# Another plan of what the attention slots of layer 0 carry: a modulation batch over three slots, queries between batches, gating weights split beside queries

## The reference, cut to what matters

```python
def _modulation(cond, w, b):
    return jnp.split(jax.nn.silu(cond) @ w + b, 6, axis=-1)      # w: 1024 x 6144, twice (x and ctx), each layer
...
def _mixer_ab(h, hc, w_in, w_out, ...):                          # layer 0
    z = h @ w_in
    q, k, v = ...                                                # 8 query heads, 2 key heads of 64; q and k with rope
    u, gv = gelu(z[..., A_IN:A_IN + B_WIDTH]), gelu(z[..., A_IN + B_WIDTH:])   # 512 + 512 columns: the gating
    a_out = _window_attention(q, k, v, kc, vc, sink)             # each block of 128 queries: 3 blocks of keys + 256 of context
    b_out = _spatial_gating(u, gv, ...)
    y = concatenate([a_out, b_out]) @ w_out
```

## Time and profile before

| what | us |
|---|---|
| median of 3 runs | 3166.69 |
| lowest and highest | 3163.51, 3169.23 |
| the profiled execution: its time | 3168.14 |
| its span | 3166.4 |
| the 40 slots and the closing one of `stage_window` | from 120.51 to about 521.4 |

### The profile page before, as it was taken

The page is one execution under the profiler, slowest core; times in us unless marked ns, Lnnn a source line. Parts: engine busy times, 40 slices in busy tenths (PEclk is TensorE's granted clock), DMA queues, the critical chain, the costliest instruction groups (busy, mean ns, idle before and its releaser), DMA issues. The chain is left out here.

```text
span 3166.4 us, 40486 instructions
## 1 busy us (share of the span) xinstructions
PE 2816.2 (89%) x15572; PEld 2300.4 (73%) x15572; DVE 1376.0 (43%) x2155; ACT 881.3 (28%) x1669; POOL 519.5 (16%) x359
## 2 busy tenths in 40 slices
PE   5877986697999999999966999999696999999993
PEld 2654865585888888888855888888575888888882
DVE  3454543564333333333364555555563333333336
ACT  4223333243121211212115434443433221122211
POOL 0000000233121121212140000000033211222114
PEclk6889998798999999999986999999998999999997
DMA  6455123542011110101023111110352111111114
GB/s 223 175 222 200 54 67 112 166 126 87 27 43 36 35 44 26 53 26 53 26 93 111 36 46 34 48 34 8 107 126 87 52 41 43 49 53 53 40 47 112
DMA packets 193647, 239.42 MB, mean 76 GB/s; under 512 B 15976, under 2 KB 154816, under 8 KB 187392
## 3 DMA queue, kind: packets, MB, share of 16 engines
q1 hardware_dynamic: 193248, 237.81, 23.3%
q10 hardware_dynamic: 288, 0.10, 0.0%
HBM read 204.22 MB, written 37.88 MB: 76 GB/s over the span
## 5 line engine op out<-in xcount | busy, mean ns | idle before, releaser
L1830 DVE TENSOR_TENSOR y<-y,pair 128x1024 f32<-128x1024 f32 x288 | 351.1, 1219 | 338.5 <-PE pair L1882 338.5
L1880 PE MATMUL pair<-m_wbh,m_ath 128*128 128x512 f32 x1152 | 449.8, 390 | 4.6 <-DVE y L1830 4.5
L1882 PE MATMUL pair<-m_wbh,m_atl 128*128 128x512 f32 x1152 | 450.3, 391 | 0.0
L1881 PE MATMUL pair<-m_wbl,m_ath 128*128 128x512 f32 x1152 | 449.3, 390 | 0.0
L1858 DVE TENSOR_TENSOR m_atl<-m_sq,m_ath 128x512 fp32r<-128x512 f32 x160 | 102.3, 640 | 696.0 <-POOL m_sq L1815 696.0
L1798 ACT ACTIVATE m_rel<-pair 128x512 f32<-128x512 f32 x160 | 88.9, 555 | 1019.9 <-PE pair L1898 1019.9
L1815 POOL TENSOR_TENSOR m_sq<-m_rel 128x512 f32<-128x512 f32 x160 | 154.1, 963 | 1214.6 <-ACT m_rel L1798 1214.6
L1896 PE MATMUL pair<-hth,m0n_wah 128*128 128x512 f32 (+1 forms) x768 | 272.8, 355 | 13.3 <-POOL m0n_wal L1808 13.3
L1897 PE MATMUL pair<-htl,m0n_wah 128*128 128x512 f32 (+1 forms) x768 | 273.3, 356 | 0.0
L1898 PE MATMUL pair<-hth,m0n_wal 128*128 128x512 f32 (+1 forms) x768 | 273.2, 356 | 0.0
L1880 PEld LDWEIGHTS pair<-m_wbh,m_ath 128*128 128x128 f32 x1152 | 216.4, 188 | 52.8 <-DVE y L1830 7.5
(11 more groups left out here) (241 smaller groups left out, 5095.5 us busy)
## 6 DMA issues: line engine op xcount, KB each, us to landing
a_ring<-in_w_mod SPq DMA_DIRECT2D x40, 1024.0 KB, 10.5
m_rawa<-in_mlp_w SPq DMA_DIRECT2D x64, 512.0 KB, 4.2
m_rawb<-in_mlp_w SPq DMA_DIRECT2D x64, 512.0 KB, 4.2
x_rows<-r_res SPq DMA_DIRECT2D x28, 512.0 KB, 3.1
r_raw<-cat_cols SPq DMA_DIRECT2D x18, 512.0 KB, 4.7
m_rawa<-x_rows SPq DMA_DIRECT2D x18, 512.0 KB, 3.7
mod_w<-in_w_mod SPq DMA_DIRECT2D x8, 1024.0 KB, 12.2
r_xin<-in_x SPq DMA_DIRECT2D x16, 512.0 KB, 3.7
```

What stands on the lines that cost most here:

```text
L1830: dve.tensor_tensor(k.y[:, t, :], k.y[:, t, :], k.pair[t % 2][:, :], ALU.add).then_inc(s_y, 1)
L1880: pe.matmul(o, ath[:, m, ts], wbh[:, m, cols], start=m == 0, stop=False)
L1881: pe.matmul(o, ath[:, m, ts], wbl[:, m, cols], start=False, stop=False)
L1882: i = pe.matmul(o, atl[:, m, ts], wbh[:, m, cols], start=False, stop=m == M - 1)
```

## The change

It replaces the tables. A batch of modulation is cut in parts of 3, 3 and 2 chunks that three slots in a row carry; `mod_rows` and the turn come in the third. The five batches start at slots 0, 4, 8, 13 and 17 (before: whole in slots 2, 7, 11, 14 and 17). The queries of the next two `it` go between the batches, at 3, 7, 11, 12, 16 and 20 (before 5, 9, 12, 15, 19, 22). The query weights are split at the ends of slots 1, 11 and 21 (before 1, 13, 23), and the gating parts at the ends of 20, 21, 30 and 31, two at each (before 18, 19, and four at 31). The gates start at slot 22 (before 20).

| slots | before | after |
|---|---|---|
| 0 to 2 | -, -, mod 1 | mod 1 in three parts |
| 3 to 7 | -, -, q, -, mod 2 | q, mod 2 in three parts, q |
| 8 to 12 | -, q, -, mod 3, q | mod 3 in three parts, q, q |
| 13 to 19 | -, mod 4, q, -, mod 5, -, q | mod 4 in three parts, q, mod 5 in three parts |
| 20 to 24 | gate, gate, q + gate, gate, gate | q, -, gate, gate + gate, gate |
| 25 to 31 | q + gate, gate, gate, gate, q, gate, q | q + gate, gate, gate, gate, q + gate, gate, q |
| 32 to 39 | ten gates, two each in 35 and 37 | ten gates, two each in 34 and 37 |

```diff
-    q_slot = {(1, 0): 5, (1, 1): 9, (1, 2): 12, (2, 0): 15, (2, 1): 19, (2, 2): 22, (3, 0): 25, (3, 1): 29, (3, 2): 31}
+    q_slot = {(1, 0): 3, (1, 1): 7, (1, 2): 11, (2, 0): 12, (2, 1): 16, (2, 2): 20, (3, 0): 25, (3, 1): 29, (3, 2): 31}
...
-    for b, n in ((1, 2), (2, 7), (3, 11), (4, 14), (5, 17)):
-        first[n], second[n] = ("mod", b), ("turn", b)
-    gates = [20, 21, -22, 23, 24, -25, 26, 27, 28, 30] + [32, 33, 34, 35, -35, 36, 37, -37, 38, 39]
+    parts = ((0, 3), (3, 6), (6, KT))
+    batch_slot = {1: 0, 2: 4, 3: 8, 4: 13, 5: 17}
+    for b, n in batch_slot.items():
+        for i, (lo, hi) in enumerate(parts):
+            first[n + i] = ("mod", b, lo, hi)
+        second[n + 2] = ("turn", b)
+    gates = [22, 23, -23, 24, -25, 26, 27, 28, -29, 30] + [32, 33, 34, -34, 35, 36, 37, -37, 38, 39]
...
-    q_splits = {1: 1, 13: 2, 23: 3}
-    gate_splits = {18: (0, 1), 19: (2, 3), 31: (4, 5, 6, 7)}
+    q_splits = {1: 1, 11: 2, 21: 3}
+    gate_splits = {20: (0, 1), 21: (2, 3), 30: (4, 5), 31: (6, 7)}
...
-    chunk_slot = lambda i: {1: 2, 2: 7, 3: 11, 4: 14, 5: 17}[i // KT + 1]
+    chunk_slot = lambda i: batch_slot[i // KT + 1] + i % KT // 3
...
-            def modulation(b):
-                for kt in range(KT):
+            def modulation(b, begin, end):
+                for kt in range(begin, end):
...
                 if f:
-                    beside_free(before)
+                    if f[0] != "mod" or f[2] == 0:
+                        beside_free(before)
```

More of the change, by code:

```diff
@@ L608, in stage_window @@
     bank_of = lambda g: k.bank[g % 4] if g < HEAD else BESIDE
-    rotated_at = {n + 1: g for n, (x, g) in ((n, f) for n, f in first.items() if f[0] == "q") if turned(g)}
+    rotated_at = {n + 1: f[1] for n, f in first.items() if f[0] == "q" and turned(f[1])}
     parted_at = {n + 1: g for n, g in rotated_at.items()}
@@ L690, in beside @@
             def beside(f):
-                kind, i = f
+                kind, i = f[0], f[1]
                 if kind == "gate":
@@ L711, in _ @@
                         chunk(i)
-                if n in first and first[n][0] == "mod":
+                if n in first and first[n][0] == "mod" and first[n][3] == KT:
                     b = first[n][1]
@@ L1145, in _ @@
                     else:
-                        modulation(f[1])
+                        modulation(*f[1:])
                 if n:
```

## The result

Two numbers for the same change:

| | before | after |
|---|---|---|
| median of 5 runs | 3163.51 us (3158.52 to 3169.23) | 3138.50 us (3134.53 to 3143.66) |
| profiled execution | 3168.14 us | 3139.57 us |

The account below looks back on a forecast made before the run. TensorE was taken as the busiest engine, with winnable idle time in slots 0 to 19 and 32. Terms -32.2 + 7.6 - 7.8 + 2.6 = -29.8 us gave 3138.3 profiled, 3137 median; range 3128 to 3153, own range 3129 to 3146.

Parts of the forecast that it names:

- Slots 0 to 19: Modulation batches in three parts and moved queries: 154.1 us against 186.3, so -32.2 us.
- The wait that takes the place of the DMA's: Part-two modulation slots: TensorE waits for VectorE's copies, behind rotate; maxima starts 2.7 us into the slot, not 1.2.
- The first slots: Slots 0 to 2: 23.9 us against 31.5, with 1.2 GHz only in slot 0 and half of slot 1.
- Slots 20 to 31: Moved gating and query splits delay maxima and gates, less slot 20's old wait: +7.6 us in sum.
- Slot 32: Gating parts 4 and 5 split a slot earlier: 13.6 us against 21.35, so -7.8 us.
- The clock in parts two and three: Ten modulation slots with idle stretches of 1.9 to 2.3 us: one clock fall in ten, +2.6 us, bounds 0 and 26.
- The rival of 18 us: Micro-idles pull the clock down in eight of ten modulation slots: 18 us given back, 3155 us; chance 0.15.
- batch 2's stretches: Old plan's modulation slot: TensorE idle stretches up to 1.87 us left the clock at 1.00; taken as evidence against falls.
- Late ring: Chunks land at the worst time and each batch keeps half its waits: 13 us, 3150 us; chance 0.12.
- slower: The clock stays at 1.2 GHz through all modulation slots: 61 us more, 3198 us; chance 0.04.
- no effect: The plan does not reach the end because another chain ends the stage: 3167 us; chance 0.04.
- One sign: If the forecast is right, DMA share is even over slots 0 to 19; before, 0.84 in a modulation slot, 0.12 beside.

Follow-up runs that it names:

- experiments 3 and 4: Modulation chunks load a quarter of their bytes, same matmuls: in the old plan 3133.72 us, in the new plan 3142.28 us.
- the other three profiles of these slots: New plan run again (3143.18 us), new plan with gating parts 4 to 7 all split at slot 31 (3146.19 us), new plan with quarter chunks (3142.28 us).
- Experiment 5: New plan with modulation chunks after the transposes and VectorE's and ScalarE's copies before normalise and exponents: 3119.23 us, ratio 0.9854 to the kernel before.
- the second set of runs: The new plan run once more, unchanged, for another profile: 3143.18 us, ratio 0.9936 to the kernel before.
- experiment 6: New plan with each modulation batch in two parts of four chunks, not three parts: 3143.78 us, ratio 0.9933 to the kernel before.
- 7 and 8: First: Experiment 5's kernel with the last query split at slot 23, not 21, 3115.37 us; second: that plus ScalarE's query split before the copy-out, 3110.76 us.

## Why the prediction was right, point by point

- **Slots 0 to 19**: forecast -32.2 and +2.6 for the clock, -29.6; measured -30.4. Shown by experiments 3 and 4: the time lost was the ring's, and the new plan is indifferent to the loads. That the number came so near is in part luck: the other three profiles of these slots give -26.6, -23.3 and -23.5, by the clock.
- **The wait that takes the place of the DMA's**, VectorE behind rotate, was named and placed right (2.05 us idle in slot 5, maxima 2.65 into the slot). Experiment 5 shows what it and the like waits of the other parts cost, with the clock that falls behind them: 21 to 25 us.
- **The first slots**: 23.9 forecast, 22.3 measured (122.05 to 144.39); the clock was back at 2.4 GHz at 127.2 instead of 132.2.
- **Slots 20 to 31**: +7.6 forecast, +8.6 measured. Slot 21 is 7.87 (7.2), slot 31 10.9 (10.1). The splits before gate 0 ended 5.1 us into slot 22 (5.3). TensorE waited 3.3 us at gate 0 and 1.9 at gate 10, not 4 and 3, because the scores before them ran at 1.2 GHz.
- **Slot 32**: 13.6 forecast, 14.7 measured; the last split ended 3.7 us into the slot (3.9), and the clock cost 2.7 us and not 1.3 (14.73 less 9.2 and the 2.8 from 405.10, where scores would end at full clock, to gate 10 at 407.89).
- **The clock in parts two and three** was the weakest term. One fall in ten was taken; the first profile has three, each of 3.4 us, and they cost 2.7 us if every slot is set against its best over the four profiles (153.1 us in all). In the three other profiles the same sum gives 6.6, 9.7 and 9.9, so the 2.6 was right for the mildest of four executions, by luck, and well under half of the cost in the others. The rival of 18 us is not reached, but it is half true. That it is also why the second set of runs gains 20 us and not 25 is likely and not isolated: the granted clock of those six runs is 0.941 to 0.944, that of the first five 0.943 to 0.948. The Trainium skill, "TensorE: Matmul & The Clock Gate", section "A second HAM failure mode: psum-queue depth-cycling", which the prediction set against batch 2's stretches, describes these runs better than the reading that I set against it: stretches of 1.7 to 2.0 us were followed by a lower clock in some executions and not in others. The stretches themselves were not all as forecast: of the ten slots that were given 1.9 to 2.3 us, slots 5, 6, 14 and 15 had 2.0, slot 2 had 3.5, and the others 1.7 or less.
- One stretch was overlooked as a danger to the clock: in slot 2 VectorE starts late for the query split (the time of the slot was right, 9.6 for 9.8), and TensorE is idle 3.5 us there. In three of the four profiles the clock fell behind it and slots 2 and 3 took 21.0 to 22.7 us instead of 18.6.
- Late ring, slower, no effect: none of them. The ring would be late with two parts (experiment 6). One sign did not come: the DMA share is not even, with 0.58, 1.00 and 0.92 in slots 4 to 6 and 0.31 in slot 12.

## What to carry to other kernels

A job whose data come from memory should be cut to what the buffer can refill in one step of the loop; the old plan wanted eight chunks where five were held, and paid 26.5 us of waits for bandwidth that lay idle beside it. A job added to a step must then go where its engine would wait anyway, and the other engines' order must follow: the same cut with the chunks after the transposes and the copies first was worth some 20 us more. And when a queue becomes dense, look for the small stores in it whose buffers something on the path needs.

## What the runs showed of the hardware that I had not expected

- Idle stretches of 1.7 to 2.0 us on TensorE, with busy slots around them, were followed by 3.4 to 6.8 us at 1.2 GHz in some executions of the same instructions and not in others; with the 3.5 us of slot 2, slots 0 to 19 took from 155.8 to 163.0 us so. Stretches of up to 1.87 us in the old plan were not followed by it in slot 7.
- With ring chunks outstanding, one of SyncE's DMA instructions for a chunk held its queue for 5.6, 5.6 and 5.9 us in experiments 5, 7 and 8, where 0.33 is usual: the two at 190.73 took 6.64 us together. A 64 KB store issued just before them took 13.6 us to free its buffer.
